# Two transformer blocks on one core: the last tile ahead of each norm and the first behind it by halves of the tokens, the last squares totalled on TensorE

## The reference, cut to what matters

```python
def rmsnorm(x, w):                     # first block
    xf = x * lax.rsqrt(jnp.mean(x * x, axis=-1, keepdims=True) + EPS)
    return xf * w

# first block, in the order of the kernel's names
x = x + merged @ w_mix_out
u = rmsnorm(x, norm_ffn_w)             # "ffn0"
up, gate = jnp.split(u @ w_ffn_up, 2, axis=-1)
x = x + (silu(causal_dwconv(up, ...)) * gate) @ w_ffn_down
x = rmsnorm(x, norm_final_w)           # end of the first block
# second block
h = modulate(rms_norm(x, g_ffn1), sh1, sc1)     # "ffn1"
x = x + 0.5 * (1 + ga1) * swiglu(h, w1_gate, w1_up, w1_down)
h = modulate(rms_norm(x, g_mix), sh2, sc2)      # "mix2"
x = x + (1 + ga2) * hybrid_mixer(h, ...)
h = modulate(rms_norm(x, g_ffn2), sh3, sc3)     # "ffn2"
x = x + 0.5 * (1 + ga3) * swiglu(h, w2_gate, w2_up, w2_down)
```

## Time and profile before

| | |
|---|---|
| median of 3 runs | 1838.52 us (1838.18 to 1839.8) |
| the profiled execution's own time | 1839.81 us |
| its span, first to last instruction | 1838.1 us |
| TensorE busy, share of the span | 99% |
| VectorE, ScalarE busy | 53%, 36% |
| granted TensorE clock, mean | 0.999 |
| HBM traffic | 109 GB/s mean |

### The profile page before, as it was taken

The page is one execution under the profiler, slowest core; times in us unless marked ns, Lnnn a source line. Parts: engine busy times, 40 slices in busy tenths (PEclk is TensorE's granted clock), DMA queues, the critical chain, the costliest instruction groups (busy, mean ns, idle before and its releaser), DMA issues. The chain is left out here.

```text
span 1838.1 us, 20910 instructions
## 1 busy us (share of the span) xinstructions
PE 1818.3 (99%) x8677; PEld 1509.8 (82%) x8677; DVE 977.3 (53%) x1341; ACT 660.5 (36%) x1004; POOL 29.7 (2%) x62
## 2 busy tenths in 40 slices
PE   9999999999999999999999999999999999999998
PEld 8788888887888888878888888788788888888887
DVE  5655453457777756674433334556757543333333
ACT  5534441334323323342222222454656332122222
POOL 0000000000000000000000000011100000000001
PEclk9999999999999999999999999999999999999999
DMA  5222233364586565323333333322121333333323
GB/s 150 79 81 81 80 87 90 90 189 154 193 260 221 189 200 186 89 81 103 92 92 92 103 92 92 82 56 58 47 58 35 92 92 92 100 96 96 100 87 97
DMA packets 321860, 200.04 MB, mean 109 GB/s; under 512 B 6712, under 2 KB 311270, under 8 KB 321766
## 3 DMA queue, kind: packets, MB, share of 16 engines
q1 hardware_dynamic: 320882, 196.31, 35.7%
q0 software_dynamic: 640, 2.10, 0.4%
q10 hardware_dynamic: 244, 0.30, 0.1%
HBM read 196.58 MB, written 2.10 MB: 108 GB/s over the span
## 5 line engine op out<-in xcount | busy, mean ns | idle before, releaser
L1422 PE MATMUL ps<-u_hi,w_hi 128*128 128x512 f32 (+1 forms) x1704 | 668.5, 392 | 4.6 <-DVE u_lo L885 1.8
L1422 PE MATMUL ps<-u_hi,w_lo 128*128 128x512 f32 (+1 forms) x1704 | 660.2, 387 | 0.0
L1422 PE MATMUL ps<-u_lo,w_hi 128*128 128x512 f32 (+1 forms) x1704 | 659.8, 387 | 0.0
L853 DVE TENSOR_TENSOR w_lo<-w_raw,w_hi 128x1024 fp32r<-128x1024 f32 (+2 forms) x307 | 364.5, 1187 | 271.3 <-ACT w_hi L435 270.3
L435 ACT ACTIVATE w_hi<-w_raw 128x1024 fp32r<-128x1024 f32 (+2 forms) x307 | 314.6, 1025 | 234.7 <-DMA w_raw<-in_w_down 80.1
L1422 PEld LDWEIGHTS ps<-u_hi,w_hi 128*128 128x128 f32 x1704 | 319.9, 188 | 78.6 <-issue 8.9
L1422 PEld LDWEIGHTS ps<-u_hi,w_lo 128*128 128x128 f32 x1704 | 319.9, 188 | 66.4
L1422 PEld LDWEIGHTS ps<-u_lo,w_hi 128*128 128x128 f32 x1704 | 320.2, 188 | 63.4 <-issue 1.2
L1422 PE MATMUL ps<-y_hi,w_hi 128*128 128x512 f32 x656 | 256.0, 390 | 0.0
L1422 PE MATMUL ps<-y_hi,w_lo 128*128 128x512 f32 x656 | 255.3, 389 | 0.0
L1422 PE MATMUL ps<-y_lo,w_hi 128*128 128x512 f32 x656 | 255.2, 389 | 0.0
(11 more groups left out here) (271 smaller groups left out, 1315.8 us busy)
## 6 DMA issues: line engine op xcount, KB each, us to landing
mod_raw<-in_w_mod SPq DMA_DIRECT2D x72, 512.0 KB, 4.8
w_raw<-in_w_in SPq DMA_DIRECT2D x71, 512.0 KB, 3.8
w_raw<-in_w_ffn_up SPq DMA_DIRECT2D x44, 512.0 KB, 4.0
w_raw<-in_w_gate SPq DMA_DIRECT2D x44, 512.0 KB, 3.8
w_raw<-in_w_up SPq DMA_DIRECT2D x44, 512.0 KB, 3.8
w_raw<-in_w_down SPq DMA_DIRECT2D x32, 512.0 KB, 3.8
w_raw<-in_w_ffn_down SPq DMA_DIRECT2D x16, 512.0 KB, 4.1
w_raw<-in_w_down SPq DMA_DIRECT2D x16, 384.0 KB, 3.4
```

What stands on the lines that cost most here:

```text
L853: e.tensor_tensor(w_lo[u % SLOTS][:, 0:n_k, :], w_raw[u % SLOTS][:, 0:n_k, :], f32(w_hi[u % SLOTS][:, 0:n_k, :]), ALU.subtract).then_inc(l ...
L1422: return e.matmul(out_, lhsT, rhs, start=start, stop=stop, skip_group_check=skip)
```

## The change

The last tile ahead of each norm (tile 7) is added and squared in two halves of 256 tokens. Its squares are no longer added to `ssum` on VectorE: TensorE adds them in PSUM, with `ones` (for ffn1 with `w2_last`, a matrix filled with the last column of `w2e`) times the squares, on top of `ones` times the sum over the first seven tiles. Each half has its own bank (7 and 6), ScalarE takes its roots by halves, and tile 0 behind the norm is scaled and cut by halves. The useless matmuls are fewer (none ahead of the total, 22 behind it; 2 in the second norm). Since bank 6 is now used by a total, the groups of `mod` are laid out anew (20, 12, 20, 20 columns instead of 20, 16, 20, 16), group 0 is turned ahead of unit 2 and reduced at tiles 2 to 6, and the plain total goes into bank 5. VectorE waits for the plain total before it scales tile 1. Left out of the diff are the declarations of the new buffer `w2_last` and of three new semaphores.

```diff
@@ -31,7 +31,7 @@
-MOD_GROUPS = ((0, 20), (20, 36), (36, 56), (56, 72))
+MOD_GROUPS = ((0, 20), (20, 32), (32, 52), (52, 72))
 MOD_BANKS = [(t1 - t0) // 4 for t0, t1 in MOD_GROUPS]
@@ -133,6 +133,8 @@
 FILL = {"mix": 0, "ffn0": 1, "ffn1": 2, "mix2": 3, "heads": 4, "ffn2": 5}
+
+N_SQ, N_SUM, N_NORM = KC + 1, KC - 1, KC + 1
 SQ = {"ffn0": 0, "ffn1": 1, "mix2": 2, "ffn2": 3}
@@ -356,6 +362,9 @@
         EPS_OF = {"mix": EPS1, "ffn0": EPS1, "ffn1": EPS1 * EPS2, "mix2": EPS2, "ffn2": EPS2}
+
+        def total_bank(h):
+            return ps[:, AUX - h, half(h)]
@@ -436,9 +445,10 @@
                 e.preload_act_table_set(LN_EXP)
-                e.wait_ge(total_done, SQ[which] + 1)
-                after_own(e.activation(rstd[:, :], bank(AUX), ACT.Ln, bias=EPS_COL[EPS_OF[which]], scale=1.0 / D_MODEL))
-                e.activation(rstd[:, :], rstd[:, :], ACT.Exp, scale=-0.5).then_inc(rstd_set, 1)
+                for h in range(2):
+                    e.wait_ge(total_done, 2 * SQ[which] + h + 1)
+                    after_own(e.activation(rstd[:, half(h)], total_bank(h), ACT.Ln, bias=EPS_COL[EPS_OF[which]], scale=1.0 / D_MODEL))
+                    e.activation(rstd[:, half(h)], rstd[:, half(h)], ACT.Exp, scale=-0.5).then_inc(rstd_set, 1)
@@ -448,21 +458,32 @@
                 f = FILL[which]
-                n0 = [FILL[n] for n in ("ffn0", "ffn1", "mix2", "ffn2")].index(f) * KC
-                for c in range(KC):
-                    e.wait_ge(normed, n0 + c + 1)
-                    e.activation(u_hi[:, c, :], t_b[c % 2][:, :], ACT.Identity,
-                                 bias=SHIFT[which](c) if SHIFT[which] else 0.0).then_inc(u_hi_set, 1)
+                shift = SHIFT[which] or (lambda c: 0.0)
+                n0 = SQ[which] * N_NORM
+                for h in range(2):
+                    e.wait_ge(normed, n0 + h + 1)
+                    ins = e.activation(u_hi[:, 0, half(h)], t_b[0][:, half(h)], ACT.Identity, bias=shift(0))
+                    ins.then_inc(first_half_hi if h == 0 else u_hi_set, 1)
+                for c in range(1, KC):
+                    e.wait_ge(normed, n0 + c + 2)
+                    e.activation(u_hi[:, c, :], t_b[c % 2][:, :], ACT.Identity, bias=shift(c)).then_inc(u_hi_set, 1)
             def residual(u0, which=None):
                 for c in range(KC):
                     u = u0 + c
                     cut_hi(u + 2)
-                    if which:
+                    if which and c >= 2:
+                        e.wait_ge(summed, SQ[which] * N_SUM + c - 1)
+                    if which and c < KC - 1:
                         e.wait_ge(bank_read[u % 2], u // 2 + 1)
-                        if c >= 2:
-                            e.wait_ge(summed, SQ[which] * KC + c - 1)
                         e.activation(t_b[c % 2][:, :], x[:, c, :], ACT.Square).then_inc(squared, 1)
+                    elif which:
+                        for h in range(2):
+                            if h == 0:
+                                e.wait_ge(x_half, SQ[which] + 1)
+                            else:
+                                e.wait_ge(bank_read[u % 2], u // 2 + 1)
+                            e.activation(t_b[c % 2][:, half(h)], x[:, c, half(h)], ACT.Square).then_inc(squared, 1)
@@ -638,7 +659,7 @@
             e.wait_ge(plain_total, 1)
-            after_own(e.activation(plain_r, bank(6), ACT.Ln, bias=EPS_COL[EPS1], scale=1.0 / D_MODEL))
+            after_own(e.activation(plain_r, bank(5), ACT.Ln, bias=EPS_COL[EPS1], scale=1.0 / D_MODEL))
             e.activation(plain_r, plain_r, ACT.Exp, scale=-0.5).then_inc(plain_root, 1)
@@ -853,8 +874,8 @@
             def add_square(which, c):
-                n = SQ[which] * KC + c
-                e.wait_ge(squared, n + 1)
+                n = SQ[which] * N_SUM + c
+                e.wait_ge(squared, SQ[which] * N_SQ + c + 1)
                 if which == "ffn1":
@@ -866,7 +887,7 @@
                     if SQ[which]:
-                        e.wait_ge(total_done, SQ[which])
+                        e.wait_ge(total_done, 2 * SQ[which])
                     e.tensor_copy(ssum[:, :], t_b[0][:, :]).then_inc(summed, 1)
@@ -874,28 +895,37 @@
                 f = FILL[which]
-                order = [FILL[n] for n in ("ffn0", "ffn1", "mix2", "ffn2")].index(f)
-                n0 = order * KC
-
-                def low(c):
-                    e.wait_ge(u_hi_set, f * KC + c + 1)
+                n0 = SQ[which] * N_NORM
+
+                def low(c, cols=slice(0, SEQ), ready=None):
+                    if ready is None:
+                        e.wait_ge(u_hi_set, f * KC + c + 1)
+                    else:
+                        e.wait_ge(*ready)
+                    dst, src, hi = u_lo[:, c, cols], t_b[c % 2][:, cols], f32(u_hi[:, c, cols])
                     if SHIFT[which] is None:
-                        e.tensor_tensor(u_lo[:, c, :], t_b[c % 2][:, :], f32(u_hi[:, c, :]), ALU.subtract).then_inc(u_lo_set, 1)
-                    else:
-                        e.scalar_tensor_tensor(out=u_lo[:, c, :], in0=t_b[c % 2][:, :], scalar=SHIFT[which](c), in1=f32(u_hi[:, c, :]),
-                                               op0=ALU.add, op1=ALU.subtract).then_inc(u_lo_set, 1)
+                        return e.tensor_tensor(dst, src, hi, ALU.subtract)
+                    return e.scalar_tensor_tensor(out=dst, in0=src, scalar=SHIFT[which](c), in1=hi, op0=ALU.add, op1=ALU.subtract)
+
+                def scaled(c, cols=slice(0, SEQ)):
+                    e.scalar_tensor_tensor(out=t_b[c % 2][:, cols], in0=x[:, c, cols], scalar=GAIN[which](c), in1=rstd[:, cols],
+                                           op0=ALU.mult, op1=ALU.mult).then_inc(normed, 1)
                 cut_lo(first_unit + 2)
-                e.wait_ge(rstd_set, SQ[which] + 1)
-                e.wait_ge(summed, SQ[which] * KC + KC)
-                for c in range(KC):
-                    if c >= 2:
-                        low(c - 2)
-                        e.wait_ge(u_lo_set, f * KC + c - 1)
-                    e.scalar_tensor_tensor(out=t_b[c % 2][:, :], in0=x[:, c, :], scalar=GAIN[which](c), in1=rstd[:, :],
-                                           op0=ALU.mult, op1=ALU.mult).then_inc(normed, 1)
-                low(KC - 2)
-                low(KC - 1)
+                for h in range(2):
+                    e.wait_ge(rstd_set, 2 * SQ[which] + h + 1)
+                    scaled(0, half(h))
+                if which == "ffn1":
+
+                    e.wait_ge(plain_total, 1)
+                scaled(1)
+                low(0, half(0), (first_half_hi, SQ[which] + 1))
+                low(0, half(1)).then_inc(u_lo_set, 1)
+                for c in range(2, KC):
+                    e.wait_ge(u_lo_set, f * KC + c - 1)
+                    scaled(c)
+                    low(c - 1).then_inc(u_lo_set, 1)
+                low(KC - 1).then_inc(u_lo_set, 1)
@@ -904,17 +934,17 @@
                         e.wait_ge(x_final, KC)
-                    if gain is None:
-                        ins = e.tensor_tensor(x[:, c, :], x[:, c, :], ubank(u), ALU.add)
-                    else:
-                        ins = e.scalar_tensor_tensor(out=x[:, c, :], in0=ubank(u), scalar=gain(c), in1=x[:, c, :], op0=ALU.mult, op1=ALU.add)
-                    ins.then_inc(bank_read[u % 2], 1)
-                    if which == "ffn1" and c >= 4:
-
-                        mod_sum(0, c - 4)
-                        if c == KC - 1:
-                            mod_sum(0, 4)
-                    if which:
+                    halves = [half(0), half(1)] if which and c == KC - 1 else [slice(0, SEQ)]
+                    for cols in halves:
+                        if gain is None:
+                            ins = e.tensor_tensor(x[:, c, cols], x[:, c, cols], ubank(u)[:, cols], ALU.add)
+                        else:
+                            ins = e.scalar_tensor_tensor(out=x[:, c, cols], in0=ubank(u)[:, cols], scalar=gain(c), in1=x[:, c, cols], op0=ALU.mult, op1=ALU.add)
+                        ins.then_inc(bank_read[u % 2] if cols is halves[-1] else x_half, 1)
+                    if which == "ffn1" and 0 <= c - 2 < MOD_BANKS[0]:
+
+                        mod_sum(0, c - 2)
+                    if which and c < KC - 1:
                         add_square(which, c)
@@ -1198,6 +1228,7 @@
             after_own(e.tensor_scalar(w2e[:, :], w2e[:, :], EPS2, None, ALU.add))
+            e.tensor_scalar(w2_last[:, :], ones[:, :], w2e[:, KC - 1:KC], None, ALU.mult).then_inc(w2_set, 1)
             ffn(0, None, "ffn1")
@@ -1465,9 +1496,14 @@
-            def total(which):
-                e.wait_ge(summed, (SQ[which] + 1) * KC)
-                mm(bank(AUX), ones[:, :], ssum[:, :], True, True).then_inc(total_done, 1)
+            def total(which, sums=ssum, last=ones):
+
+                e.wait_ge(summed, (SQ[which] + 1) * N_SUM)
+                for h in range(2):
```

(27 more changed lines are left out.)

## The result

The changed kernel takes 1845.14 us (median of 7 runs, 1843.54 to 1851.25) against 1838.52 us (1838.18 to 1841.38): a ratio of 1.0037, 95% interval 1.0028 to 1.0047.

What follows compares the result with a forecast made beforehand. It took ScalarE's cut and table load to bound the norms, with TensorE busy 99% of the span. Norms -0.86 us and `mod` +0.43 gave -0.4 us: 1838.1 us from 1838.52, range 1836.2 to 1840.0 (8 in 10).

Steps and rivals of the forecast that it cites:

- What bounds the kernel: At the fourth norm, 7.59 us without useful work; ScalarE's cut and table load mostly hide the sum and total.
- Halves: At each norm, halves cost 0.6 of a whole; gains 0.09 to 0.15 us at addition, 0.02 to 0.07 at roots.
- Sum and total on TensorE: Behind each norm's last tile: squares' total 1.5 us earlier, worth nothing; only the second norm gains its wait, 0.16 us.
- The columns of `mod`: Group 3's four more transposes, where TensorE is the bound, cost 0.43 us more; the other groups nothing.
- `keep_busy`: Ahead of the first product: TensorE idle 2.9 us in three norms, 2.1 in the second; costs nothing if clock stays.
- the 0.98 us on which I leaned: Longest idle piece at full pace in the trace before; did no harm, taken as evidence against a fall of the clock.
- the rival's band of 1845 to 1848 us: Idle pieces behind norms lower TensorE's clock, losing about 2.3 us each in three or four norms; chance 0.11.

Runs made afterwards that it cites:

- c_both: Changed kernel with the table load moved ahead into a pause and the strip's cut moved behind the norm: 1833.83 us, ratio 0.9974.
- b_both: Kernel before with the table load moved ahead into a pause and the strip's cut moved behind the norm: 1837.26 us, ratio 0.9995.
- filled kernel: Changed kernel with 42 instead of 22 useless matmuls in three norms and 16 instead of 2 in the second: 1838.21 us, ratio 0.9997.
- c_table: Changed kernel with the table load alone moved ahead, and 30 (second norm 6) useless matmuls: 1832.17 us, ratio 0.9966.
- b_gap: Kernel before with 12 instead of 28 useless matmuls behind the total in the first, third and fourth norm: 1843.21 us, ratio 1.0021.
- a_mid: Changed kernel with 32 instead of 22 useless matmuls in the first, third and fourth norm: 1838.71 us, ratio 0.9999.
- a_whole: The filled kernel without halves: last tile, total, roots and first tile whole, last squares still added on TensorE: 1839.51 us, ratio 1.0003.
- d_28: c_both with 28 instead of 22 useless matmuls, and 4 instead of 2 in the second norm: 1831.86 us, ratio 0.9956.
- d_gate: d_28 with four useless matmuls added behind the 8-column matmuls ahead of the attention: 1831.79 us, ratio 0.9962.
- a_fill: The filled kernel: 42 instead of 22 useless matmuls in three norms, 16 instead of 2 in the second, against the changed kernel: 1838.21 us.

## Why the prediction was wrong, point by point

*What bounds the kernel.* Right. ScalarE's instructions stand back to back in all four norms of the profile after, and clearing them out of the way shortens the gaps to 5.5 to 5.6 us (c_both) while the change alone does not.

*Halves.* Right in size: 0.75 us for the four gaps, 0.86 forecast, and the rows of 256 columns were the right price.

*Sum and total on TensorE.* Right: nothing in the changed kernel beyond the wait in the second norm. b_both against c_both shows the 1.6 to 2.2 us for each norm that it brings once ScalarE is out of the way, the halves' 0.15 included. The whole total is ready 1.1 us earlier than before and not the 1.5 us of the sum (2.18 us behind the last addition's start instead of 3.32), which cost nothing here.

*The columns of `mod`.* Right: from the second to the third norm the filled kernel takes 0.43 us more than the one before, the price of four transposes.

***`keep_busy`* is the step that failed.** I had worked out the idle piece (2.9 and 2.1 us forecast, 2.5 to 2.6 and 2.0 measured) and what a fall of the clock would cost, and then entered the piece into the sum at zero, with a chance of 0.11 that it would not be. In its place the runs show: with the pieces filled 1838.21 us, where I had forecast 1838.1 for the change as a whole; with them left idle 1845.14, with the granted clock at 0.50 for 3.4 us behind three norms; and in the kernel before, such pieces alone bring 1843.21.

Two readings led me there. First, I took a mean granted clock of 0.999 for a clock that never fell. A fall of 3.4 us to one half lowers the mean over 1838 us by 0.0009, so 0.999 leaves room for one fall and doesn't say where it is. In the filled kernel's profile, with the same mean, the only fall stands behind TensorE's last matmul, where it costs nothing:

```profile
1833.00:1834.00 1.00, 0.00 (x0) 0.00 (x0) 0.00 (x0) 0.00 (x0) 0.07 (x1) 0.50 0.73 217
```

The trace of before has its fall in the midst of the work, in a place where TensorE is idle for no more than 0.1 us, as its windows show:

```profile
1194.00:1195.00 1.00, 1.00 (x12) 1.00 (x12) 0.00 (x0) 0.00 (x0) 0.00 (x0) 1.00 0.67 116
...
1196.00:1197.00 1.00, 1.00 (x6) 0.67 (x5) 0.49 (x2) 0.52 (x3) 0.00 (x0) 0.50 0.28 81
1197.00:1198.00 1.00, 1.00 (x8) 1.00 (x10) 0.27 (x1) 0.56 (x1) 0.00 (x0) 0.50 0.00 0
```

Just ahead of it TensorE works on matmuls of eight columns and then on eight transposes:

```profile
1193.53 0.59 PE L1422 MATMUL ps<-gate,ones 128*128 128x8 f32 x4
...
1194.20 0.81 PE L1422 MATMUL ps<-gate,ones 128*128 128x8 f32 x6
...
1195.09 0.63 PE L1425 MATMUL ps<-consts,t_a 128*128 128x128 f32 x4
1195.81 1.11 PE L1425 MATMUL ps<-consts,f_wide 128*128 128x128 f32 x4
```

So the clock can fall even without an idle piece, and the 0.98 us on which I leaned (the longest at full pace is in fact 1.06 us, ahead of 1415.56) was no evidence for pieces three times as long. Second, between a piece known to be harmless and a cold start known to be slow I had no row, which speaks for even chances and not for one in nine. The Trainium skill, "TensorE: Matmul & The Clock Gate", section "Why this matters for your kernels", warns of idle gaps between bursts of matmuls and so spoke against the change; the trace agrees with its direction, but pieces shorter than the gap it calls harmful were enough, 2.49 us in the first norm and 1.97 in one profile of the second.

That the time lies in the rival's band of 1845 to 1848 us is partly luck. Its mechanism was right, but its price of 2.3 us for each fall was too high (0.95 to 1.5 measured): I had taken the low pace to last some 5 us, and it lasted 3.4. Three falls at the measured price give 1841 to 1843 us; 1845 came out because a late strip, and a fourth fall behind it, came beside the three. In the profile of the changed kernel, against the filled one: 1.4 us in the first stretch, 4.7 in the third (a fall of the third norm's size, the late strip and the fall behind it), 1.0 at the end and 0.1 at the start, together the 7.1 us between the spans of 1836.3 and 1843.4. Even the fastest of the seven executions took 1843.54 us, more than three falls explain; how the late strip and the falls share the time of the other runs stays open; their mean clocks of 0.992 to 0.997 speak for several falls in each (0.0009 for one).

## What to carry to other kernels

When an edit shortens the work that TensorE does while it waits, lay out what is left as one idle piece and price the clock's fall at even chances unless a row of the same length speaks against it; here three idle pieces of 2.5 to 2.6 us cost more than the whole edit gave. Read the granted clock in windows and not as a mean: 0.999 over 1838 us can hide a fall of 3.4 us. And an operand that comes earlier is worth nothing while the engine that takes it has other work queued ahead; here the earlier total gave nothing alone, and clearing ScalarE's queue in the kernel before gave 1 us (b_both), while with the earlier total in place moving the table load into a pause gave 6 us (c_table).

## What the runs showed of the hardware that I had not expected

- The clock's fall depends on more than the length of the idle piece: 2.83 us did nothing in one norm of b_gap, and 2.66 and 2.84 us brought a fall in the others; 1.97 us brought one in a_mid and none in the changed kernel.
- A run of 20 matmul records of eight columns and eight transposes, with TensorE hardly idle, was followed by a fall in seven of eleven profiles (before, a_mid, a_whole, c_both, c_table, d_28 and d_gate) and not in those of after, a_fill, b_gap and b_both. Which of the two instructions it goes with, and why it isn't there every time, isn't shown. It costs 1.5 us (291.38 against 289.91 in the table). Most executions of the kernel before lie near 1838.2 or near 1839.7 us, which this fall would explain: the profiled one, with the fall, took 1839.81.
- The load of one and the same strip of the w_o units landed about 2 us later in two of eleven profiles (ScalarE waited 2.66 us in after and 2.74 in c_both, 0.45 to 0.71 in the other nine), with the same issue behind it. I haven't found out why.
